# Reordering the entries of the two modulated mixers, their FFNs and the step behind the second gate in a two-network float32 kernel

## The chip, the cores and the metric

The kernel runs on one core of a Trainium2 chip. The metric is the device time of one execution in microseconds (us); the time before is the median of 3 runs. Engines: TensorE (PE, its weight loads PEld), VectorE (DVE), ScalarE (ACT), GpSimd (POOL), and SyncE (SP), which issues the weight transfers.

## The reference

`x` is 512 tokens by 1024. A first network of two layers (half FFN, mixer, half FFN, gate) ends in `rmsnorm(x, final_norm)`; its output is the input of a second network of two layers with modulated norms:

```python
gate = jax.nn.sigmoid(rmsnorm(x, ple_norm[layer]) @ ple_gate[layer])
x = x + gate * (p[layer] @ ple_proj[layer])
...
return rmsnorm(x, final_norm)
# second network, per layer
mod = (c_act @ w_ada[l] + b_ada[l])[:, None, :]
sh1, sc1, g1, sh2, sc2, g2 = jnp.split(mod, N_MOD, axis=-1)
h = rmsnorm_2(x, norm1_w[l]) * (1.0 + sc1) + sh1
x = x + g1 * hybrid_mixer(h, ...)
h = rmsnorm_2(x, norm2_w[l]) * (1.0 + sc2) + sh2
x = x + g2 * swiglu_2(h, w_gate_up[l], w_down[l])
```

## The kernel before

`x` lies in SBUF as 8 tiles of 128 features by 512 tokens. Each float32 product is made of three passes over high and low parts: weights arrive as raw chunks (`raw`, 3 buffers), ACT copies the rounded high part (`wh`), DVE subtracts for the low part (`wl`); both have 3 buffers, so weight tile i can be split only when tile i-3 is used up (`step`). Activations are split in the same way into `hh` and `hl`. Each engine runs one hand-written program in order; a wait on it holds all that stands behind it.

The stages that matter here, in order: `ple 1` (the second gate), `final` (last norm of the first network), `mix2 0`, `ffn2 0`, `mix2 1`, `ffn2 1`. Between stages PE does not wait for the norm. A norm's gain is put into `G`; the first products of the next stage run on `x*G` without the root of the mean square (`gained`), and the root is applied afterwards.

- A second-network mixer is entered by `entered`: four weight tiles T 0 to T 3 (424 columns), each against four token tiles (24 matmuls per weight tile). Meanwhile the squares of x are summed over features by one-column matmuls (`token_means`, 16 of them), DVE copies the sums (`token_roots`), POOL takes the power -0.5 (`roots`, `rtok`), PE spreads the root over the partitions (`along`), and DVE and ACT make eight normed tiles (`modulated`: T from x, G and the root; `hh`; `hl`), which overwrite the gained ones. On DVE, `entered` does the splits for T 0 and T 1 (which reach up to T 3, two ahead) before the copy of the sums, and the split for T 2 (up to the first `xb` tile) before the normed tiles.
- At the entry of `mix2 0` two roots are taken: of the final norm's input (`rtok`, key `al`) and of its output (`r2`, key `al2`, from the squares with the final gain in T1). The final root goes into `R`, and DVE scales the eight tiles of x by it (`rescaled`) inside the mixer's body.
- An FFN of the second network is entered by `opened`: its first two products (w1 0, w1 1) interleaved over the eight gained tiles, with the sums, a two-column product `c` and `along` between them; the third product (w3 0) runs on the normed tiles. The split of w3 1 comes behind the eight normed tiles, in `ffn`.
- `shifted` sums the weight columns times the shift on DVE (for the mixer two per T tile, for the FFN eight in one go).
- `ple` ends with `project`, the additions to x (`add`), the squares and the gained tiles.

The order of the work is the order of the code in each engine's program; there is no planner. Weight transfers are issued by SP when the chunk three before is split.

Of the kernel before, what the change touches and what calls it, by code (L numbers as in the profile page):

```python
# [166 lines left out]
def build(nc, I, out):  # L167
    with ExitStack() as ctx:
# [296 lines left out]
        def pe_program(e):  # L465
# [106 lines left out]
            def entered(s):  # L572
# [3 lines left out]
                for q in range(4):  # L576
# [3 lines left out]
                    for t, b in enumerate(bs):  # L580
                        r = slice(128 * t, 128 * t + 128)
                        for j in range(2):
                            k = 2 * q + j
                            operand((s, "h0"), k)
                            pe.mm(b[:, 0:424], hh[:, k, r], lo[:, j, :], k == 0, False)
                            pe.mm(b[:, 0:424], hl[:, k, r], hi[:, j, :], False, False)
                            done = pe.mm(b[:, 0:424], hh[:, k, r], hi[:, j, :], False, k == 7)
                    done.then_inc(used, g)
                    pe.advance()
                    yield q  # L590
# [6 lines left out]
            def opened(s, names):  # L597
# [7 lines left out]
                for k in range(8):  # L605
# [8 lines left out]
                    if k == 2:  # L614
                        token_means(s)
                    if k == 4:
# [4 lines left out]
                    if k == 5:  # L621
# [3 lines left out]
            def enter(s):  # L625
# [11 lines left out]
                if s[0] == "mix2":  # L637
                    for q in entered(s):
                        if q == 0:
                            token_means(s)  # L640
                        if q == 1:
# [86 lines left out]
            def final(s, nxt):  # L728
                for q in entered(nxt):
                    if q == 1:  # L730
# [4 lines left out]
                    if q == 2:  # L735
                        pe.wait_ge(pooled, ("r2", s))
                        along(("al2", s), r2)
                        pe.wait_ge(pooled, ("rtok", s))
                        along(("al", s), rtok)
# [193 lines left out]
            def mix2(s, nxt):  # L933
# [260 lines left out]
                for j in range(4):  # L1194
# [4 lines left out]
                    done.then_inc(formed, (s, "cat", j))  # L1199
                rest = begin(s, [("out", 0), ("out", 1)], ch, cl, (s, "c"), (0, 1, 2, 3))  # L1200
# [41 lines left out]
        def act_program(e):  # L1242
# [109 lines left out]
            def enter(s):  # L1352
# [16 lines left out]
                for t in range(8):  # L1369
                    modulated(s, 3, t)  # L1370
# [58 lines left out]
            def ple(s, nxt):  # L1429
# [3 lines left out]
                for k in range(8):  # L1433
                    product(s, "gate", k)
                    if k == 7:
                        normed(nxt, 0)
# [12 lines left out]
                for t in (1, 2, 3):  # L1449
                    normed(nxt, t)  # L1450
                squares(nxt, 6)
                for t in (4, 5):
                    normed(nxt, t)
                squares(nxt, 7)
                for t in (6, 7):
                    normed(nxt, t)
                enter(nxt)

            def final(s, nxt):
                entered(nxt)  # L1460
                act.wait_ge(formed, ("al", s))
                act.f(R[:, :], ps(("al", s))[:, :], ACT.Copy).then_inc(left(("al", s)), ("al", s))
# [202 lines left out]
            def mix2(s, nxt):  # L1665
# [216 lines left out]
                for j in range(4):  # L1882
                    act.wait_ge(formed, (s, "cat", j))
                    part((s, "c", j), ps((s, "cat", j))[:, :], ch[:, j, :])
                begin(s, [("out", 0), ("out", 1)])
# [51 lines left out]
        def dve_program(e):  # L1937
# [4 lines left out]
            def shifted(g):  # L1942
# [4 lines left out]
                src = raw_view(n)  # L1947
                for t in rows:
# [14 lines left out]
            def step(g):  # L1963
# [6 lines left out]
                while at[0] < len(order):  # L1970
# [116 lines left out]
            def enter(s):  # L2087
# [17 lines left out]
                for t in modulated(s, 3, R[:, :]):  # L2105
                    pass
# [66 lines left out]
            def out_product(s, nxt, gate=None, rest=False):  # L2173
# [4 lines left out]
                for t in range(8):  # L2178
                    product(s, "out", t)
                    dve.wait_ge(used, G_of[(s, "out", t)])  # L2180
# [6 lines left out]
                    after(nxt, t)  # L2187
                enter(nxt)

            def ple(s, nxt):  # L2190
# [12 lines left out]
                if nxt[0] == "final":  # L2203
# [3 lines left out]
                    dve.tt(G[:, :], G[:, :], cols("final_norm", 0, 8), MUL).then_inc(worked, (to, "G"))  # L2207
                for k in range(8):
                    product(s, "gate", k)
# [13 lines left out]
                    for t in {4: (0, 1), 5: (2, 3), 6: (4, 5)}.get(k, ()):  # L2223
                        add(t)
                        add_square(nxt, t)
                normed = norm_tile if nxt[0] in DEFERRED else gained
# [334 lines left out]
            def mix2(s, nxt):  # L2561
# [36 lines left out]
                if l == 0:  # L2598
                    for t in range(4):
                        rescaled(t)  # L2600
# [22 lines left out]
                if l == 0:  # L2623
                    for t in range(4, 8):
                        rescaled(t)
# [551 lines left out]
```

## Time and profile before

| | us |
|---|---|
| median of 3 runs | 3360.82 (3358.36 to 3363.05) |
| the profiled execution's own time | 3360.46 |
| its span in the profile | 3358.7 |
| PE busy | 3285.3 (98%) |
| DVE busy | 1820.4 (54%) |
| ACT busy | 1167.6 (35%) |
| POOL busy | 74.2 (2%) |

The granted TensorE clock was 0.99 of full on average. PE is busy nearly all the time, so the change can act only on the short stretches where PE is idle or runs at the lower clock. A matmul's busy time overlaps the next one's; the pace is the distance between starts: 0.23 us for 512 columns and 0.19 us for 424 at the full clock.

### The profile page before, as it was taken

Reading aid. Unit: us, or ns where it says so; the run is one execution under the profiler, and the core shown is the slowest. Engines: PE = TensorE matmul, PEld = TensorE weight load, DVE = VectorE, ACT = ScalarE, POOL = GpSimd, SP = SyncE. Lnnn points to the kernel's source line nnn. Section 1 sums busy time; section 2 is a strip of 40 time slices with the busy share of each in tenths; the row PEclk is TensorE's granted clock in tenths of the full one; section 3 lists DMA queues with packets and bytes.
Section 4 is the critical chain, followed back from the end, with each engine's and each line's share of the span. In section 5 each row is a group of like instructions: output and inputs, shape, how many; then the busy total and the mean of one; then the engine's idle time right before and its main releaser. Section 6 shows DMA issues by size and latency. Waiting matters only on the chain.

```text
span 3358.7 us, 37181 instructions
## 1 busy us (share of the span) xinstructions
PE 3285.3 (98%) x15371; PEld 2714.2 (81%) x15371; DVE 1820.4 (54%) x2593; ACT 1167.6 (35%) x1621; POOL 74.2 (2%) x100
## 2 busy tenths in 40 slices
PE   7999999999999999999999999999999999999999
PEld 6888876888888888887888888887788888878887
DVE  5664356566436664366566545876433368563332
ACT  4322253322233222263332224553322245442221
POOL 1000000000000000000000001100000010000000
PEclk9999999999999999999999999999999999999999
DMA  5443321444333443322244332211232322022322
GB/s 152 140 139 121 104 86 51 132 134 148 116 116 101 151 138 116 99 86 76 88 140 149 132 107 84 85 38 38 88 100 86 103 87 76 1 77 99 101 94 69
DMA packets 334142, 339.86 MB, mean 101 GB/s; under 512 B 12182, under 2 KB 329048, under 8 KB 333976
## 3 DMA queue, kind: packets, MB, share of 16 engines
q1 hardware_dynamic: 332696, 333.98, 30.6%
q0 software_dynamic: 1280, 3.50, 0.4%
q8 instruction: 124, 2.03, 0.2%
q14 instruction: 42, 0.34, 0.0%
HBM read 335.36 MB, written 2.10 MB: 100 GB/s over the span
## 4 chain that ended last, share of the span: by engine, by line
PE 62%; DVE 5%; ACT 2%; issue 1%; DVEq 0%; ACTq 0%
PE ps L135 60%; PE ps L138 2%; DVE hl L108 1%; DVE wl L100 1%; DVE ar L100 1%; DVE ar L108 1%; DVE T L108 1%; ACT hh L95 0%; ACT wh L95 0%; DVE ar L117 0%; DVE ada L108 0%; ACT ch L95 0%; ACT ar L95 0%; DVE ar L104 0%; DVE x L100 0%
## 5 line engine op out<-in xcount | busy, mean ns | idle before, releaser
L135 PE MATMUL ps<-hh,wl 128*128 128x512 f32 x2760 | 1091.9, 396 | 30.5 <-DVE wl L100 13.4
L135 PE MATMUL ps<-hl,wh 128*128 128x512 f32 x2760 | 1077.5, 390 | 0.0
L135 PE MATMUL ps<-hh,wh 128*128 128x512 f32 x2760 | 1077.4, 390 | 0.0
L100 DVE TENSOR_TENSOR wl<-raw,wh 128x1024 fp32r<-128x1024 f32 (+2 forms) x547 | 654.0, 1198 | 771.6 <-ACT wh L95 771.3
L95 ACT ACTIVATE wh<-raw 128x1024 fp32r<-128x1024 f32 (+2 forms) x547 | 560.4, 1027 | 481.6 <-PE ps L135 466.8
L135 PEld LDWEIGHTS ps<-hh,wl 128*128 128x128 f32 x2760 | 520.7, 189 | 152.8 <-issue 33.4
L135 PEld LDWEIGHTS ps<-hh,wh 128*128 128x128 f32 x2760 | 520.1, 188 | 110.1
L135 PEld LDWEIGHTS ps<-hl,wh 128*128 128x128 f32 x2760 | 521.1, 189 | 104.1 <-issue 0.6
L135 PE MATMUL ps<-uh,wl 128*128 128x512 f32 x1056 | 411.8, 390 | 0.0
L135 PE MATMUL ps<-uh,wh 128*128 128x512 f32 x1056 | 410.9, 389 | 0.0
L135 PE MATMUL ps<-ul,wh 128*128 128x512 f32 x1056 | 410.8, 389 | 0.0
L95 ACT ACTIVATE uh<-T 128x512 fp32r<-128x512 f32 x132 | 83.5, 633 | 474.6 <-DVE T L100 474.6
L135 PEld LDWEIGHTS ps<-uh,wh 128*128 128x128 f32 x1056 | 198.2, 188 | 41.5
L135 PEld LDWEIGHTS ps<-ul,wh 128*128 128x128 f32 x1056 | 198.2, 188 | 41.0
L135 PEld LDWEIGHTS ps<-uh,wl 128*128 128x128 f32 x1056 | 198.2, 188 | 40.5
L100 DVE TENSOR_TENSOR T<-ps,R 128x512 f32<-128x512 f32 x196 | 134.1, 689 | 121.3 <-PE ps L135 108.1
L95 ACT ACTIVATE T<-T 128x512 f32<-128x512 f32 (+1 forms) x92 | 56.0, 615 | 352.7 <-DVE T L100 352.7
L108 DVE SCALAR_TENSOR_TENSOR ada<-raw,small,ada 128x256 f32<-128x256 f32 x336 | 162.9, 485 | 12.0
L100 DVE TENSOR_TENSOR ul<-T,uh 128x512 fp32r<-128x512 f32 x132 | 91.5, 693 | 92.3 <-ACT uh L95 92.3
L95 ACT ACTIVATE ar<-ar 128x2048 f32<-128x2048 f32 (+6 forms) x68 | 73.2, 1090 | 131.5 <-DVE ar L100 101.8
L135 PE MATMUL ps<-ch,wl 128*128 128x512 f32 x256 | 103.3, 404 | 13.8 <-DVE cl L100 10.3
L135 PE MATMUL ps<-ar 128*128 128x64 f32 (+9 forms) x756 | 111.7, 315 | 4.0 <-DVE ar L108 1.9
(226 smaller groups left out, 2733.2 us busy)
## 6 DMA issues: line engine op xcount, KB each, us to landing
raw<-in_ffn_w SPq DMA_DIRECT2D x120, 1024.0 KB, 5.1
raw<-in_w_ada SPq DMA_DIRECT2D x48, 1024.0 KB, 5.2
raw<-in_w_gate_up SPq DMA_DIRECT2D x44, 1024.0 KB, 5.0
raw<-in_m_w_in SPq DMA_DIRECT2D x26, 1024.0 KB, 5.6
raw<-in_w_down SPq DMA_DIRECT2D x16, 1024.0 KB, 5.2
raw<-in_ffn_w SPq DMA_DIRECT2D x16, 768.0 KB, 4.4
raw<-in_w_in SPq DMA_DIRECT2D x12, 1024.0 KB, 5.3
raw<-in_m_w_out SPq DMA_DIRECT2D x8, 1024.0 KB, 5.2
```

What stands on the lines that cost most here:

```text
L95: return self.issue(lambda e: e.activation(out, in_, func, **kw))
L100: return self.issue(lambda e: e.tensor_tensor(out, a, b, op))
L108: return self.issue(lambda e: e.scalar_tensor_tensor(out=out, in0=a, scalar=s, in1=b, op0=op0, op1=op1))
L135: return self.issue(lambda e: e.matmul(out, l, r, start=start, stop=stop, skip_group_check=True))
L138: return self.issue(lambda e: e.transpose(out, in_, ident))
```

## The change

Five edits. (1) In `opened`, the sums, `c` and the root's spread stand behind k = 0, 1 and 2 of the two products instead of 2, 4 and 5. (2) In the FFN's entry the split of w3 1 stands at normed tile 5 instead of behind tile 7. (3) In the mixers' entries the sums stand after two token tiles of T 0 (mix2 1) or of T 1 (mix2 0), and the root's spread at the end of that weight tile; before, one weight tile later. (4) The end of `ple` is reordered, and for `mix2 0` the shift sums of T 0 to T 3 move into it. (5) The spread of the final root and the scaling of x move from `mix2 0`'s entry and body to its output product, one x tile ahead of each addition.

```diff
@@ PE: entered
+                        if t < 3:
+                            yield q, t
                     done.then_inc(used, g)
                     pe.advance()
-                    yield q
+                    yield q, 3
@@ PE: opened
-                    if k == 2:
+                    if k == 0:
                         token_means(s)
-                    if k == 4:
+                    if k == 1:
                         b = banks.take((s, "c"))
...
-                    if k == 5:
+                    if k == 2:
                         pe.wait_ge(pooled, ("rtok", s))
                         along(("al", s), rtok)
@@ PE: enter
-                    for q in entered(s):
-                        if q == 0:
+                    for at in entered(s):
+                        if at == (0, 1):
                             token_means(s)
-                        if q == 1:
+                        if at == (0, 3):
                             pe.wait_ge(pooled, ("rtok", s))
                             along(("al", s), rtok)
@@ PE: final
-                for q in entered(nxt):
-                    if q == 1:
+                for at in entered(nxt):
+                    if at == (1, 1):
                         token_means(s)
...
-                    if q == 2:
+                    if at == (1, 3):
                         pe.wait_ge(pooled, ("r2", s))
                         along(("al2", s), r2)
-                        pe.wait_ge(pooled, ("rtok", s))
-                        along(("al", s), rtok)
@@ PE: mix2, behind the cat transposes
+                if l == 0:
+                    along(("al", ("final",)), rtok)
@@ ACT: enter (and DVE alike, behind its tile 5)
                 for t in range(8):
+                    if t == 5:
+                        step(G_of[(s, "w1", 1)])
                     modulated(s, 3, t)
@@ ACT: ple
-                        normed(nxt, 0)
+                        for t in range(2):
+                            normed(nxt, t)
...
-                for t in (1, 2, 3):
+                for t in (2, 3):
                     normed(nxt, t)
-                squares(nxt, 6)
-                for t in (4, 5):
-                    normed(nxt, t)
-                squares(nxt, 7)
                 for t in (6, 7):
+                    squares(nxt, t)
+                for t in range(4, 8):
                     normed(nxt, t)
@@ DVE: shifted, step
+                dve.wait_ge(raw_in[n % RAW], n)
...
-                        if o[1] in shift_of:
+                        if o[1] in shift_of and shift_of[o[1]][0] != ("mix2", 0):
                             shifted(o[1])
@@ DVE: out_product
+                    if s == ("mix2", 0):
+                        if t == 0:
+                            rescaled(0)
+                        dve.wait_ge(x_new, (("final",), t))
...
                     after(nxt, t)
+                    if s == ("mix2", 0) and t < 7:
+                        rescaled(t + 1)
@@ DVE: ple
+                    if nxt[0] == "final" and 3 < k < 7:
+                        for q in {4: (0,), 5: (1,), 6: (2, 3)}[k]:
+                            shifted(G_of[(normed_by(nxt), "T", q)])
+                normed(nxt, 1)
+                step(G_of[(s, "gate", 7)])
+                dve.advance()
+                for t in (2, 3):
                     normed(nxt, t)
                 add(6)
-                for t in (4, 5):
-                    normed(nxt, t)
+                add(7)
                 add_square(nxt, 6)
-                add(7)
-                for t in (6, 7):
+                for t in range(4, 8):
                     normed(nxt, t)
@@ DVE: mix2 (and the same for tiles 4 to 7)
-                if l == 0:
-                    for t in range(4):
-                        rescaled(t)
```

How the order of instructions moves, at the three places that matter most.

PE at the entry of `mix2 1`, around the spread of the root (`ident,small`; `wh_63`, `wh_61` and `wh_62` are the high parts of T 0, T 1 and T 2). Before:

```order
L135 MATMUL ps<-wh_61,hl 128x424
L135 MATMUL ps<-wh_61,hh 128x424
L135 MATMUL ps<-ident,small 128x128 x4
L135 MATMUL ps<-wl_65,hh 128x424
L135 MATMUL ps<-wh_62,hl 128x424
```

After:

```order
L135 MATMUL ps<-wh_63,hl 128x424
L135 MATMUL ps<-wh_63,hh 128x424
L135 MATMUL ps<-ident,small 128x128 x4
L135 MATMUL ps<-wl_64,hh 128x424
L135 MATMUL ps<-wh_61,hl 128x424
```

The spread stands behind T 0 and ahead of T 1; before it stood behind T 1. DVE's and ACT's order at this entry is unchanged.

DVE at the end of `ple 1` and in the entry of `mix2 0` (`ada` is a shift sum, `hl` a gained tile's low part, `T_82` the last gate product times its root, `wl_65` the low part of T 1):

```order
+L108 SCALAR_TENSOR_TENSOR ada<-raw_58,mod,ada 128x424 x4
+L108 SCALAR_TENSOR_TENSOR hl<-x,G,hh 128x512
+L100 TENSOR_TENSOR T_82<-ps,R 128x512
+L108 SCALAR_TENSOR_TENSOR hl<-x,G,hh 128x512
 L100 TENSOR_TENSOR wl_65<-raw_60,wh_62 128x848
-L100 TENSOR_TENSOR T_82<-ps,R 128x512
-L108 SCALAR_TENSOR_TENSOR hl<-x,G,hh 128x512 x4
+L108 SCALAR_TENSOR_TENSOR hl<-x,G,hh 128x512 x2
```

Two gained tiles now stand ahead of T 1's split, the first of them ahead of the gate product's T as well, and the shift sums of T 2 and T 3 stand ahead of all of them; before, the split and T came first.

DVE in the output product of `mix2 0`, from the second x tile to the splits behind it (`x<-x,VT,R` is the scaling by the final root, `x<-ps,mod,x` the addition). Before:

```order
L108 SCALAR_TENSOR_TENSOR x<-ps,mod,x 128x512
L108 SCALAR_TENSOR_TENSOR hl<-x,G,hh 128x512
L108 SCALAR_TENSOR_TENSOR acc<-acc,sq_77 128x512
L100 TENSOR_TENSOR wl_65<-raw_59,wh_62 128x1024
L100 TENSOR_TENSOR wl_66<-raw_60,wh_63 128x1024
```

After:

```order
L108 SCALAR_TENSOR_TENSOR x<-x,VT,R 128x512
L108 SCALAR_TENSOR_TENSOR x<-ps,mod,x 128x512
L108 SCALAR_TENSOR_TENSOR hl<-x,G,hh 128x512
L108 SCALAR_TENSOR_TENSOR acc<-acc,sq_77 128x512
L108 SCALAR_TENSOR_TENSOR x<-x,VT,R 128x512
L100 TENSOR_TENSOR wl_65<-raw_59,wh_62 128x1024
L100 TENSOR_TENSOR wl_66<-raw_60,wh_63 128x1024
```

A scaling stands ahead of the addition, and another ahead of the two weight splits.

## Rows read from the trace of the kernel before

**Rows 1.** The page's first part: busy time and share of each engine.

```profile
PE 3285.3 (98%) x15371; PEld 2714.2 (81%) x15371; DVE 1820.4 (54%) x2593; ACT 1167.6 (35%) x1621; POOL 74.2 (2%) x100
```

**Rows 2.** Timeline, `mix2 0` entry: start, duration, instruction, idle before it and releaser.

```profile
2083.27 0.39 PE L135 MATMUL ps<-ch,ul 128*128 128x512 f32 x1
...
2088.33 0.74 DVE L108 SCALAR_TENSOR_TENSOR hl<-x,G,hh 128x512 fp32r<-128x512 f32 x1
2089.22 0.43 PE L135 MATMUL ps<-wl,hh 128*128 128x424 f32 x1 [3.07 <-DVE hl L108]
...
2102.64 1.93 PE L135 MATMUL ps<-ones,T 128*128 128x1 f32 x16
...
2107.27 0.16 DVE L111 COPY small<-ps 128x4 f32<-128x4 f32 x1
2107.57 2.14 POOL L100 TENSOR_TENSOR small<-small 128x4 f32<-128x4 f32 x2 [11.72 <-DVE small L111]
2111.27 1.95 PE L135 MATMUL ps<-ident,small 128*128 128x128 f32 x16
2112.36 1.41 DVE L108 SCALAR_TENSOR_TENSOR T<-x,G,ps 128x512 f32<-128x512 f32 x2 [3.51 <-PE ps L135]
...
2128.72 3.52 PE L138 MATMUL ps<-ident,ar 128*128 128x128 f32 x16 [1.89 <-DVE ar L108]
```

**Rows 3.** Timeline, `mix2 1` entry.

```profile
2727.63 0.91 ACT L95 ACTIVATE wh<-raw 128x848 fp32r<-128x848 f32 x1 [0.46 <-PE ps L135]
2729.66 1.36 DVE L108 SCALAR_TENSOR_TENSOR ada<-raw,mod,ada 128x424 f32<-128x424 f32 x2
2731.89 0.15 DVE L111 COPY small<-ps 128x4 f32<-128x4 f32 x1
2732.19 1.01 POOL L100 TENSOR_TENSOR small<-small 128x4 f32<-128x4 f32 x1 [373.86 <-DVE small L111]
2733.83 1.05 PE L135 MATMUL ps<-ident,small 128*128 128x128 f32 x8
2736.33 1.40 DVE L108 SCALAR_TENSOR_TENSOR T<-x,G,ps 128x512 f32<-128x512 f32 x2
```

**Rows 4.** Timeline, `ffn2 0` entry.

```profile
2351.62 0.47 PE L135 MATMUL ps<-hh,wl 128*128 128x512 f32 x1 [0.93 <-DVE wl L100]
2354.40 1.22 DVE L100 TENSOR_TENSOR wl<-raw,wh 128x1024 fp32r<-128x1024 f32 x1 [0.20 <-ACT wh L95]
2357.01 0.16 DVE L111 COPY small<-ps 128x4 f32<-128x4 f32 x1 [1.39 <-PE ps L135]
2361.46 1.05 PE L135 MATMUL ps<-ident,small 128*128 128x128 f32 x8
2363.18 1.41 DVE L108 SCALAR_TENSOR_TENSOR T<-x,G,R 128x512 f32<-128x512 f32 x2 [2.84 <-ACT R L95]
...
2372.68 1.63 DVE L108 SCALAR_TENSOR_TENSOR hl<-T,mod,hh 128x512 fp32r<-128x512 f32 x2
...
2378.64 0.76 PE L135 MATMUL ps<-hh,wl 128*128 128x512 f32 x1 [3.24 <-DVE wl L100]
```

**Rows 5.** Windows: length, busy PE, PEld, DVE, ACT, POOL, granted clock, DMA.

```profile
2378.60:2381.60 3.00, 2.96 (x7) 2.40 (x8) 2.30 (x3) 1.34 (x2) 0.00 (x0) 0.52 0.61 203
2752.70:2757.00 4.30, 4.30 (x20) 3.77 (x21) 4.08 (x6) 4.26 (x6) 1.76 (x2) 0.60 0.46 138
1043.70:1048.00 4.30, 4.30 (x27) 3.83 (x27) 1.74 (x2) 2.61 (x3) 0.00 (x0) 1.00 0.01 4
```

**Rows 6.** Timeline, scaling of x in `mix2 0`'s body, then its output product.

```profile
2132.71 2.73 DVE L108 SCALAR_TENSOR_TENSOR x<-x,VT,R 128x512 f32<-128x512 f32 x4
...
2321.15 2.36 DVE L100 TENSOR_TENSOR wl<-raw,wh 128x1024 fp32r<-128x1024 f32 x2
2322.53 0.47 PE L135 MATMUL ps<-ch,wl 128*128 128x512 f32 x1 [0.51 <-DVE wl L100]
```

**Rows 7.** Timeline, entry of the FFN behind `ple 0`.

```profile
1043.70 0.47 PE L135 MATMUL ps<-hh,wl 128*128 128x512 f32 x1 [1.74 <-DVE hl L108]
```

More of the change, by code:

```diff
@@ L1460, in final @@
                 entered(nxt)
-                act.wait_ge(formed, ("al", s))
-                act.f(R[:, :], ps(("al", s))[:, :], ACT.Copy).then_inc(left(("al", s)), ("al", s))
             def root(key, n):
@@ L1884, in mix2 @@
                     part((s, "c", j), ps((s, "cat", j))[:, :], ch[:, j, :])
+                if l == 0:
+                    key = ("al", ("final",))
+                    act.wait_ge(formed, key)
+                    act.f(R[:, :], ps(key)[:, :], ACT.Copy).then_inc(left(key), key)
                 begin(s, [("out", 0), ("out", 1)])
@@ L2105, in enter @@
                 for t in modulated(s, 3, R[:, :]):
-                    pass
+                    if t == 5:
+                        step(G_of[(s, "w1", 1)])
             def output():
@@ L2207, in ple @@
                     dve.tt(G[:, :], G[:, :], cols("final_norm", 0, 8), MUL).then_inc(worked, (to, "G"))
+                normed = norm_tile if nxt[0] in DEFERRED else gained
                 for k in range(8):
-                    product(s, "gate", k)
+                    if k < 7:
+                        product(s, "gate", k)
+                    else:
+                        normed(nxt, 0)
                     dve.wait_ge(used, G_of[(s, "gate", k)])
@@ L2222, in ple @@
                             dve.tt(cl[:, c, :], ps((s, "pt", c))[:, :], ch[:, c, :].bitcast(F32), SUB).then_inc(lo_part, (s, "p", c))
-                    for t in {4: (0, 1), 5: (2, 3), 6: (4, 5)}.get(k, ()):
+                    pair = {4: (0, 1), 5: (2, 3), 6: (4, 5)}.get(k, ())
+                    for t in pair:
                         add(t)
+                    for t in pair:
                         add_square(nxt, t)
-                normed = norm_tile if nxt[0] in DEFERRED else gained
-                for t in range(4):
+                    if nxt[0] == "final" and 3 < k < 7:
[5 more added lines that the diff above has]
+                for t in (2, 3):
                     normed(nxt, t)
                 add(6)
-                for t in (4, 5):
-                    normed(nxt, t)
+                add(7)
                 add_square(nxt, 6)
-                add(7)
-                for t in (6, 7):
+                for t in range(4, 8):
                     normed(nxt, t)
@@ L2597, in mix2 @@
                 convolved(0)
-                if l == 0:
-                    for t in range(4):
-                        rescaled(t)
                 for c in (2, 0, 1):
@@ L2622, in mix2 @@
                 conv_from(1)
-                if l == 0:
-                    for t in range(4, 8):
-                        rescaled(t)
                 step(G_of[(s, "qu", 0)])
```

## The prediction

> **What bounds the kernel now.** I read the page first: TensorE is busy for 98% of the span [rows 1], so a change of order can win only where TensorE idles or runs at half clock. Then I read, per engine, the timeline of each stretch that the diff touches, looking at the idle time before each matmul and what ended it. There are five such stretches.
>
> In the entry of `mix2 0`, TensorE starts the last two projections at 2083.27 (12 matmuls of 0.23 us, so 2.7 us), then idles 3.07 us for the first gained tile, is slow a little later, and idles again for 1.89 us until 2128.72, where DVE's T rows are missing; these hang on the normed tiles, and the normed tiles on the root, which TensorE spreads only at 2111.27 [rows 2]. In the entry of `mix2 1` the same chain runs from the split of T 3 to the root and the normed tiles [rows 3]. In the entries of the two FFNs the root is spread at 2361.46, the first normed tile is begun at 2363.18, the eighth is done at about 2374.3, and the fourth product starts only at 2378.64 after 3.24 us idle, since its low part is split behind the normed tiles [rows 4]; the second FFN repeats this pattern. Behind the first gate there is one idle stretch of 1.74 us [rows 7].
>
> **The clock.** Two idle stretches were followed by half clock: 3.24 us idle by a granted clock of 0.52 over 3 us, and 1.89 us idle (after a stretch of small waits) by 0.60 over 4.3 us. After 1.74 us idle it stayed 1.00 [rows 5]. So I count a new idle stretch of 2 us or more with 0 to 1.7 us of slow matmuls on top (0.48 x 3.0 = 1.4, 0.40 x 4.3 = 1.7), a long one with the whole.
> The Trainium skill (TensorE: Matmul & The Clock Gate, HAM oscillation — how this bites in real kernels) says that the clock falls after long idle gaps of TensorE, not short ones. By that rule only the long gap of part 3 would carry the surcharge and the sum below would be about 2 us lower; the row at 1.89 us speaks against taking it so.
>
> **1, FFN entries (edits 1 and 2), twice.** TensorE's work stays. The sums come after k = 0. Two interleaved products cost 6 x 0.23 = 1.36 us per k. From the start at 2351.6 the sums could begin at 2352.4, and wait some 0.4 us for the last square. DVE copies them behind its split of w3 0, which lasts from 2354.40 to 2355.6 [rows 4], so at 2355.7 instead of 2357.01; POOL needs 1.0 us [rows 3], so the root is there at 2357, before TensorE gets to the spread behind k = 2 (2352.8 + 1.7 sums + 2 x 1.36 + 0.4 for c = 2357.7). The spread is then 3.7 us earlier than 2361.46, and the first normed tile starts at 2359.5. Eight tiles at 1.32 us each (from 2363.18 to 2374.3 [rows 4]) now contain the split of w3 1, 1.2 us. They end at 2371.7. TensorE ends the two opened products at 2365.6, catches up with tiles 5 to 7, and is done with w3 0 at 2372.5; w3 1 is split by then. It starts 6.1 us earlier than 2378.64 and without the half clock (1.7 us): -7.8 us. Bounds: -5.5 (a spread only as much earlier as the copy, 1.3 us, still removes the 3.24 idle and its clock, 0.6 from shorter waits) to -8.5. Next in line is w1 2's split, behind two activations, some 2 us ahead of its use. For both FFNs: -15.6 us.
>
> **2, mix2 0's entry (edits 3 and 4).** The last gate product ends at 2083.27, when the gained tiles may be written. ACT takes 0.7 us for each and DVE 0.74 [rows 2]; with two of them ahead of the split of T 1, the low parts are there by 2084.9 and 2086.1, and TensorE, done with the projections at 2086.0, goes on without the 3.07 us. T 0 ends at 2090.9. T 1 up to its second tile ends at 2093.2; 8 square sums and 8 more of T1 follow, 1.7 + 1.9 us [rows 2], then two tiles, 2.3 us: 2099.2. Here it wants r2. DVE has four gained tiles and the splits of T 2 and T 3 ahead of the copy; I get the copy at 2098.8 instead of 2107.27, then POOL 2.1 us and 0.3 of latency [rows 2]: 2101.3. So 2.2 us idle, a new wait. The spread of one root (0.9 of the 1.95 us, the other moves) ends at 2102.3, and the normed tiles start 10.0 us earlier than 2112.36. T 2 and T 3 are over by 2111.8 (2113.3 with slow matmuls), so the tiles' buffers come free in time. The transposes now at 2128.72 start at 2118.6, -10.1 us, and run at 1.6 to 3.2 us instead of 3.2, of which I take -1.2. The moved spread comes back in the mixer with 0.9 us of TensorE time. Together -10.4 us. Bounds: -6 (the copy 4 us later than I count) to -12.
>
> **3, mix2 1's entry (edit 3).** DVE's and ACT's order is unchanged there: the copy of the sums stands behind the split of T 3, and T 3's buffer is free only when T 0 is used up. Now TensorE asks for the root at exactly that moment. The way from there is 0.2 + 0.91 (ACT) + 2.23 (DVE from 2729.66 to the copy) + 0.3 + 1.01 (POOL) + 0.1 = 4.8 us [rows 3]. Before, T 1's 24 matmuls (4.7 us) covered it; now TensorE idles. It also waits 0.7 us for the last square, since the sums come 2.3 us earlier, and the spread (0.8 us from 2733.83, half of the two spreads' 1.95) is now ahead of T 1's end. T 1's end frees the buffer of the xb tile, whose split stands ahead of the normed tiles: 2733.83 to 2736.33 [rows 3]. So the normed tiles, and with them the whole chain to the transposes, come 4.8 + 0.7 + 0.8 = 6.3 us later, and 1.7 us more by the half clock: +8.0 us. Bounds: +6.3 to +8.5; 0 if the root were there.
>
> **4, the scaling in the output product (edit 5).** 8 x 0.68 = 5.4 us of DVE [rows 6] leave the body, where TensorE waited for nothing of theirs: 0. In the output product the first is hidden under the wait for the first product. The next two (1.33 us) stand ahead of the split that TensorE already waits for until 2322.53 [rows 6]: +1.3 us, an idle stretch of 2.2 us. DVE then catches up, 1.2 us per product. The last two stand ahead of w1 1's split, for which TensorE waits until 2351.62 [rows 4]: +1.3 us, and 2.3 us idle with 0.6 more for the square behind it. Clock: 0 to 3.4, I take 2.4, the second being likelier. +5.0 us; bounds 0 (DVE has slack) to +6.
>
> **5, behind the first gate (edit 4).** The idle 1.74 us [rows 7] is split up: w1 1's low part now stands behind two gained tiles and comes 0.8 us late, and tiles 4 to 7 behind the last addition make TensorE wait 1.3 us at k = 4. +0.2 us; bounds -1.0 to +1.5.
>
> **Sum.** -15.6 - 10.4 + 8.0 + 5.0 + 0.2 = -12.8 us against the profiled execution's own 3360.46 (span 3358.7 and 1.8 around it), which is 0.36 below the median 3360.82. So 3360.8 - 12.8 = 3348.0 us.
>
> **Rivals.**
> - A, the second mixer's wait is covered (chance 0.11): if the copy could pass T 3's split, -20.8 us, 3340. For it: before, the root was ready 0.5 us ahead of need. Against it: the copy stands behind the split on an in-order engine.
> - B, DVE's slack absorbs the scalings (0.13): -17.8 us, 3343. For it: DVE is busy 54% [rows 1]. Against it: the two splits named are already what TensorE waits for.
> - C, the first mixer's root comes late (0.15): four gained tiles, two splits and the POOL additions of squares are all ahead of the copy, and each us of delay shifts the chain by one. With 4 to 5 us, 3352.5.
> - D, slower (0.05): the normed tiles overwrite gained ones that the opened products still read. If the `hh` writes had to wait until those are over, the earlier root would bring nothing in both FFNs: no 15.6 us, +2.8 us, 3363.6. It decides once the eighth tile ends after 2373.5 plus 3 us of w3 1's split. Against it: PE reports each k as it is used, and the root reaches DVE when k = 3 is over.
>
> The forecast itself has 0.56, own range 3344 to 3352.
>
> **Range and chances.** 0.2% (6.7 us, below 3354.1) is what a measurement of this kernel can tell from no change. Forecast, A and B are faster (0.80), of C about a quarter is (0.04), and the rest of C and a stray case are same (0.11); D is slower (0.05). The range 3340 to 3355 leaves out the far end of A and all of D.
>
> **What would show it.** Right: an idle stretch of 4 to 5 us before `ident,small` in `mix2 1`'s entry, released by POOL, with the transposes behind it some 8 us later in the stage; one of about 2 us before it in `mix2 0`'s; w3 1 without idle before it; idle of 2 us or more before the output product's fourth tile and w1 1 in `mix2 0`, and the old 0.9 in `mix2 1`. Wrong: any of the FFN entries still idle behind w3 0, or the normed tiles of `mix2 0` less than 6 us earlier.

## The result and the profile after

The changed kernel takes 3366.2 us (median of 17 runs, 3364.3 to 3370.9) against 3360.4 us for the kernel before (17 runs on the same chip): ratio 1.0019, 95% interval 1.0012 to 1.0027. I forecast 3348.0 us and a range of 3340 to 3355. It is no faster; by the bound of 0.2% it counts as the same, and the interval says slightly slower.

The page of the changed kernel, first part, beside [rows 1]:

```profile
PE 3292.2 (98%) x15371; PEld 2725.7 (81%) x15371; DVE 1823.2 (54%) x2593; ACT 1167.1 (35%) x1621; POOL 75.8 (2%) x100
```

PE is busy 6.9 us longer with the same number of instructions: the loss shows first as slower matmuls. The span went from 3358.7 to 3364.6 us, and I split it at fixed rows of PE's timeline. The second column is the kernel before; "FFN only", "bank", "root back", "scaling back", "both back" and "k = 1" are experiments of the next section. Lengths in us:

```
stage                              before  after   FFN    bank   root  scaling both   k = 1
                                                   only          back  back    back
start to spread in ple 1           2046.1  2046.6  2049.1 2044.5 2046.1 2046.0 2050.0 2045.2
... to T 0 of mix2 0                 43.2    41.7    43.2   41.7   41.7   41.7   41.7   41.7
T 0 to end of transposes             42.7    44.0    42.1   37.8   43.1   38.8   38.8   38.8
body of mix2 0                      168.0   171.9   171.5  168.2  171.7  171.6  171.6  171.6
output product of mix2 0             50.0    51.5    50.4   51.5   53.3   51.1   51.0   51.0
ffn2 0 to T 0 of mix2 1             373.0   371.3   367.3  370.3  370.3  367.4  367.4  365.2
T 0 to end of transposes, mix2 1     32.4    40.7    32.8   40.7   32.2   40.6   31.6   33.2
body of mix2 1                      170.5   169.8   170.5  169.8  170.4  169.9  167.8  170.6
output product of mix2 1             50.9    50.7    50.5   50.7   51.1   50.6   51.1   50.0
ffn2 1 to the end                   382.1   376.3   376.2  376.3  376.3  376.3  376.3  374.1
```

Three of these stages (the start and both bodies) move by 3 to 6 us between profiled executions of identical code: "FFN only" has the code of before in the first two and shows 2049.1 and 171.5 us where before has 2046.1 and 168.0. Together they are 3.8 us longer in the profile after, 6.5 in "FFN only" and 2.9 in "k = 1". What moves in them is time at half clock. The body of `mix2 0` as a window of its own, in the kernel before, after, and in "FFN only" (the last columns are granted clock, DMA share and GB/s):

```profile
2131.89:2299.87 167.98, 166.92 (x987) 140.01 (x985) 125.59 (x213) 89.76 (x188) 6.56 (x8) 0.98 0.16 50
2132.35:2304.26 171.91, 170.75 (x995) 144.01 (x993) 124.66 (x208) 92.86 (x192) 6.94 (x8) 0.96 0.14 44
2134.34:2305.83 171.49, 170.45 (x987) 143.29 (x985) 126.95 (x213) 90.54 (x189) 6.56 (x8) 0.96 0.16 50
```

0.02 of 170 us is 3.4 us, nearly the whole difference of 3.5 and 3.9. Why one execution gets more of it than another stays open, and so does whether an edit further ahead can bring it about. I read every edit in the other stages, which scatter less but not by nothing: the output product of `mix2 0` took 50.0 to 51.1 us with the code of before, and 51.5 and 53.3 us with the changed code ("root back" has half clock there behind the same idle 2.0 us). In these stages together the changed kernel is 2.1 us longer, not 12.8 shorter.

Over the whole span the mean granted clock fell from 0.990 to 0.986: TensorE stood at half clock for 68 us before and for 92 us after. Half of the 24 us more, 12 us, is the most that this can have cost. By stage it is 7.3 us more in the entry of `mix2 0`, 6.4 in its body, 6.8 in `ffn2 0`, 5.1 in the entry of `mix2 1`, and 1.7 less in the rest.

In `mix2 0`'s entry after the change (PE, DVE and POOL of the timeline):

```profile
2083.91 3.60 DVE L108 SCALAR_TENSOR_TENSOR ada<-raw,mod,ada 128x424 f32<-128x424 f32 x4
2087.42 0.75 DVE L108 SCALAR_TENSOR_TENSOR hl<-x,G,hh 128x512 fp32r<-128x512 f32 x1
2088.32 0.43 PE L135 MATMUL ps<-wl,hh 128*128 128x424 f32 x1 [1.59 <-DVE hl L108]
...
2102.27 0.15 DVE L111 COPY small<-ps 128x4 f32<-128x4 f32 x1
2102.57 2.12 POOL L100 TENSOR_TENSOR small<-small 128x4 f32<-128x4 f32 x2 [6.26 <-DVE small L111]
2106.52 1.05 PE L135 MATMUL ps<-ident,small 128*128 128x128 f32 x8
2109.02 1.40 DVE L108 SCALAR_TENSOR_TENSOR T<-x,G,ps 128x512 f32<-128x512 f32 x2
...
2122.88 2.35 DVE L108 SCALAR_TENSOR_TENSOR ar<-ps,small,ar 128x424 f32<-128x424 f32 x4
2123.58 0.79 PE L135 MATMUL ps<-hh,wl 128*128 128x512 f32 x1 [6.03 <-DVE ar L108]
```

Against [rows 2] the root does come earlier (the copy at 2102.27 instead of 2107.27, the normed tiles at 2109.02 instead of 2112.36). Then the first xb product waits 6.03 us, an idle stretch that the kernel before does not have, and its releaser is DVE's first copy of a T tile out of PSUM, which is no operand of it: it looks like a wait for a PSUM bank, and experiments 1 and 2 test that. The transposes follow at 2130.69, later than the 2128.72 of before.

PE in the output product of the first mixer and in the second mixer's entry, after the change:

```profile
2328.47 0.47 PE L135 MATMUL ps<-ch,wl 128*128 128x512 f32 x1 [2.00 <-DVE wl L100]
...
2358.87 0.66 PE L135 MATMUL ps<-hh,wl 128*128 128x512 f32 x1 [2.27 <-DVE wl L100]
...
2739.02 2.08 PE L135 MATMUL ps<-ident,small 128*128 128x128 f32 x8 [4.56 <-POOL small L100]
...
2766.10 1.94 PE L138 MATMUL ps<-ident,ar 128*128 128x128 f32 x16 [1.90 <-DVE ar L108]
```

Here the predicted waits are there: 4.56 us for POOL's root, and 2.00 and 2.27 us for low parts where [rows 6] and [rows 4] have 0.51 and 0.93. The old 3.24 us ahead of the fourth product are gone. The granted clock (the figure behind POOL) of three windows:

```profile
2102.20:2106.50 4.30, 4.30 (x13) 4.04 (x14) 0.38 (x3) 0.00 (x0) 3.20 (x5) 0.51 0.58 187
2123.50:2127.00 3.50, 3.42 (x8) 2.74 (x9) 2.93 (x5) 0.00 (x0) 3.03 (x7) 0.52 0.00 0
2356.00:2370.00 14.00, 11.73 (x43) 9.69 (x42) 5.59 (x9) 3.01 (x4) 1.01 (x1) 0.63 0.23 75
```

The second and third hold what follows the idle 6.03 and 2.27 us. The first follows no idle stretch but 32 one-column sums, behind which the kernel before has half clock too, for half as long (windows after, then before):

```profile
2099.60:2106.40 6.80, 6.80 (x26) 6.54 (x26) 2.98 (x6) 1.51 (x2) 3.20 (x5) 0.50 0.37 118
2105.00:2108.40 3.40, 3.36 (x10) 3.18 (x11) 3.21 (x6) 0.00 (x0) 0.83 (x1) 0.50 0.00 0
```

### The profile page after: what moved, and what is told of

It is laid out like the page before. It is cut to its first block, busy times and chain, and to the rows that moved or that the text cites. A ratio compares the mean times of both kernels' runs of the same rounds, so it can differ in the third digit from the quotient of the medians.

```text
span 3364.6 us, 37195 instructions
## 1 busy us (share of the span) xinstructions
PE 3292.2 (98%) x15371; PEld 2725.7 (81%) x15371; DVE 1823.2 (54%) x2593; ACT 1167.1 (35%) x1621; POOL 75.8 (2%) x100
## 4 chain that ended last, share of the span: by engine, by line
PE 89%; DVE 7%; ACT 2%; issue 1%; DMA 0%; SPq 0%; POOL 0%; DVEq 0%; ACTq 0%; POOLq 0%
PE ps L135 88%; PE ps L138 2%; DVE wl L100 1%; DVE ar L100 1%; DVE hl L108 1%; DVE ar L108 1%; ACT wh L95 1%; DVE T L108 1%; ACT ar L95 0%; ACT hh L95 0%; DVE ada L108 0%; DVE ar L117 0%; ACT ch L95 0%; DMA raw<-in_ffn_w 0%; DVE ar L104 0%
```

## The experiments

**1. One bank further.** The kernel has 8 PSUM banks handed out in turn. Edit 5 takes one spread out of the entry, and with it one turn of this rotation: the first xb product, on bank 3 before, is now on bank 5, where T 0 lies until DVE has copied it behind all normed tiles. The experiment turns the rotation on by six at that place and changes nothing else of the changed kernel:

```diff
                         along(("al2", s), r2)
+                banks.turn += 6
```

> The changed kernel (span 3364.6) with one line more in TensorE's program: behind the root's spread in mix2 0's entry six PSUM banks are skipped, so that the first xb product takes the bank of the square sums (ps3), as in the kernel before, and not T 0's (ps5), which DVE empties only behind all normed tiles. Theory (bank): the idle stretch of 6.03 us ahead of that product goes; the product is then paced by the normed tiles, which end at 2122.4, and the transposes come at about 2125.3 instead of 2130.7: 5 to 6 us less in this stage, whole kernel about 3361. Rival (the wait is for the normed tiles or T rows themselves): no change of the place of the transposes, whole kernel about 3366.

Measured: 3357.54 us, ratio to before 0.9993 (0.9984 to 1.0002), by the ratios 8.7 us less than the changed kernel. The transposes in PE's timeline:

```profile
2122.22 1.94 PE L138 MATMUL ps<-ident,ar 128*128 128x128 f32 x16 [1.89 <-DVE ar L108]
```

The stage from T 0 to their end is 37.8 us instead of 44.0: the bank is worth 6.2 us here. The idle 1.89 us ahead of the transposes are those of before.

**2. The bank in the kernel before.** Two runs turn the rotation in the kernel before, where nothing else is changed. In the first I miscounted: by seven banks the product falls on the bank of the second spread, which ACT empties, and not on T 0's.

```diff
                         pe.wait_ge(pooled, ("rtok", s))
                         along(("al", s), rtok)
+                banks.turn += 7    # the second run: += 2
```

> The kernel before with nothing changed but the rotation of the PSUM banks: seven banks are skipped behind the first mixer's last spread, so that the first xb product takes the bank it takes in the changed kernel, T 0's. Theory, the bank alone makes the wait: xb starts when DVE has copied T 0, at some 2126.9 us instead of 2118.6 us, TensorE is idle for about 8 us, the transposes behind it start at 2134 us instead of 2128.7 us and, since their operands are then long there, run at 1.9 us instead of 3.5 us; the stage from the row to the body is 18 to 19 us long instead of 14.2, +4 to +5 us in all, 3365 us. Rival, the wait for DVE in the changed kernel comes from the earlier root or from DVE's new order and not from the bank: no idle stretch there, and the time of before.

> The kernel before with nothing changed but the rotation of the PSUM banks: two banks are skipped behind the first mixer's last spread, so that the first xb product takes T 0's bank and the four transposes the banks that they take in the changed kernel. Theory, T 0's bank alone makes the wait: DVE begins its four copies of T at 2126.2 us as before, xb starts some 0.7 us behind that instead of at 2118.6 us, after 8 us of idle time released by DVE; its 24 matmuls take 7.1 us as in the changed kernel, the transposes start at 2134 us instead of 2128.7 us and take 1.6 us less: the stage from the row to the body is 18 us long instead of 14.2 (16.7 with the spread's bank), +3.8 us, 3364 us. Rival, DVE does not release it: the stage stays at 14.2 us.

Measured: 3363.93 us with seven (1.0007, 0.9999 to 1.0016), 3371.20 us with two (1.0032, 1.0020 to 1.0044), where I had expected 3364. The first xb product in PE's timeline, in the one and in the other:

```profile
2125.31 0.80 PE L135 MATMUL ps<-hh,wl 128*128 128x512 f32 x1 [6.95 <-ACT R L95]
```

```profile
2127.58 0.79 PE L135 MATMUL ps<-hh,wl 128*128 128x512 f32 x1 [8.38 <-DVE ar L108]
```

With T 0's bank the product waits for DVE's copy in the kernel before too, and the stretch from the row product (`ada,small`, behind T 3) to the body grows from 14.2 to 19.4 us (16.7 with the other bank). So a late bank alone makes the wait, without the earlier root or DVE's new order; the rest of that run's 9.9 us lies outside the entry, 3.5 of it in the body that scatters.

**3. The second mixer's root put back** (sums and spread one weight tile later, the changed kernel otherwise).

```diff
-                        if at == (0, 1):
-                            token_means(s)
                         if at == (0, 3):
+                            token_means(s)
+                        if at == (1, 3):
                             pe.wait_ge(pooled, ("rtok", s))
```

> The changed kernel with the sums and the root's spread of mix2 1's entry put back by one weight tile (sums behind T 0, spread behind T 1). Theory: the copy of the sums stands behind T 3's split, which waits for T 0's end; the 4.6 us idle ahead of the spread goes, with the half clock behind it, and the stage is 8 us shorter (3358 for the whole). Rival (the earlier spread pays back part of it further on, in the mixer's body): under 6 us.

Measured: 3354.58 us (0.9988, 0.9979 to 0.9998). T 0 to the row product is 21.19 us again, as before, against 29.43: edit 3 costs 8.2 us there, and I had said 8.0. The rival, a part paid back further on, did not appear: the stage to the end of the transposes is 32.2 us, with 32.4 before.

**4. The FFN entries alone** (edits 1 and 2 in the kernel before), then each of the two alone.

> The kernel before with edits 1 and 2 alone (sums, c and spread at k = 0, 1, 2 of the opened products; split of w3 1 at normed tile 5). Theory: both FFN entries gain what the second one gained in the changed kernel, 5.9 us each, since w1 1's idle time ahead of the sums is 0.9 us as there: 3360.4 - 11.8 = 3348.6. Rival (the half clock that the changed kernel shows over 10 us in the first FFN's entry comes from the early one-column sums, not from the longer idle time that edit 5 makes): the first FFN gains under 3 us, 3351.5 or more.

> The kernel before with edit 1 alone: in the FFN entries the sums follow k = 0, c follows k = 1, the spread k = 2; w3 1's split stays behind all eight normed tiles. Theory, root and split are two links of one chain: the tiles start about 3.5 us earlier and w3 1's split with them, and TensorE is done with w3 0 only 1 to 2 us earlier, so the idle 3.24 us shrinks to 1 or less: -3.5 us for each FFN, -7.0 us, 3353.8 us. Rival, the earlier root is worth nothing while the split stands behind the tiles: 0 to -2 us.

> The kernel before with edit 2 alone: w3 1's split stands ahead of normed tile 5 on ACT and DVE, the root stays at its old place. Theory: w3 1 starts without its 3.24 us of idle time and the half clock behind it, but tiles 5 to 7 come 1.2 us later and TensorE, which follows them, with them: -3.2 us for each FFN, -6.4 us, 3354.4 us. If -3.5 and -3.2 add up to more than the 5.7 measured for both edits, each of the two alone removes most of the idle stretch and its half clock, which I had counted whole beside the earlier root. Rival, the split alone does it all and the earlier root nothing: -5.7 for each FFN, 3349.4 us.

Measured: both 3352.76 us (0.9974, 0.9965 to 0.9984); sums alone 3362.98 (0.9997, 0.9988 to 1.0007); split alone 3359.05 (0.9995, 0.9986 to 1.0004). By the stages of `ffn2 0` and `ffn2 1` both edits save 5.6 and 5.9 us, the sums alone 0.7 and 0.6, the split alone 2.2 and 3.9 (I had expected 3.2 each, and 3.5 each for the sums). The medians show less: for both edits I had expected 3348.6 us. Four of the ten executions took 3345.7 to 3346.8 us at a mean granted clock of 0.990, the other six 3351.9 to 3355.7 us at 0.987 or 0.988, so the scatter that goes with the clock shows within one kernel too. My expectation for the sums alone fell: the tiles start 1.9 us earlier, but the idle stretch keeps its whole length, since the split of w3 1 starts behind the last tile whenever that is, and the matmuls behind it are slow for longer. From PE's timeline and the windows of that run:

```profile
2382.71 0.76 PE L135 MATMUL ps<-hh,wl 128*128 128x512 f32 x1 [3.23 <-DVE wl L100]
```

```profile
2361.00:2366.00 5.00, 5.00 (x21) 4.22 (x20) 0.83 (x3) 0.00 (x0) 1.01 (x1) 0.66 0.18 60
2382.70:2388.00 5.30, 5.29 (x13) 4.13 (x14) 3.52 (x4) 1.58 (x2) 0.00 (x0) 0.50 0.60 198
```

The window from 2361 shows the other half of the story: the clock is 0.66 right behind the one-column sums. Experiment 7 takes that up.

**5. The scaling put back** (edit 5 undone: the final root's spread again beside the other one, `rescaled` again in the body).

```diff
                         along(("al2", s), r2)
+                        pe.wait_ge(pooled, ("rtok", s))
+                        along(("al", s), rtok)
```

> The changed kernel without edit 5: the final root is spread right behind r2 in mix2 0's entry and x is scaled in the mixer's body. This also moves the bank rotation back by one, so the xb product does not take T 0's bank. Theory: the bank wait goes (5 to 6 us), the output product loses its two longer idle stretches (2.9 us), the spread in the half-clock stretch behind the cat transposes goes (2.0, of which 0.9 comes back in the entry) and the first FFN's entry gains 3 us more: 3366 - 12.5 = 3353.7. Rival (DVE's 5.4 us in the body now delay something, or the half clock stays in the first FFN's entry): 3357 or more.

Measured: 3354.28 us (0.9986, 0.9976 to 0.9995). I had expected 3353.7 us. This also restores the bank rotation, so its 11 us less than the changed kernel (by the ratios) hold both: T 0 to the transposes' end is 38.8 us instead of 44.0, and `ffn2 0` 4.0 us shorter.

**6. Both put back, and the shift sums.** The changed kernel without edit 5 and with the second mixer's root at its old place; and the same with only two of the four shift sums moved into `ple`.

```diff
-                        for q in {4: (0,), 5: (1,), 6: (2, 3)}[k]:
+                        for q in {4: (0,), 5: (1,), 6: ()}[k]:
```

> The changed kernel without edit 5, and with the sums and the spread of the second mixer's entry back at their old places (the first mixer's entry and both FFN entries stay changed). Theory, each cost hangs on its own stage: the entry of `mix2 0` keeps the 5.3 us of the earlier root since the second spread moves the rotation of the PSUM banks on, the second mixer's entry is 8 us shorter than in the changed kernel, the output product loses its two idle stretches (4 us); both FFN entries keep 5.7 us each. Sum against the kernel before: -0.6 (behind ple 1) - 4.7 - 11.4 = -16.7 us, 3342.5 us. Rival, the stages trade with each other (half clock that goes in one comes back in the next, as the 64-column part of the first mixer's body already does by 3.5 us): 3347 to 3350 us.

> The kernel of the run above, with the shift sums of T 2 and T 3 back at those tiles' splits and only those of T 0 and T 1 ahead in `ple`. Theory, DVE's 3.60 us of four shift sums ahead of the first gained tile are what makes hl 2.5 us later than I predicted: two of them gone, the gap of 1.59 us before T 0 goes, and the way from the last projections to T 0 is about 1.6 us shorter, and the copy of the sums is not later, since TensorE's sums come after T 1's tiles: 1 to 1.6 us less than the run above. Rival, DVE's queue between T 0 and the copy of the sums is what sets the root: the two shift sums come back ahead of the copy, the root is 1.8 us later and the time is the same or up to 1 us more.

Measured: 3344.23 us (0.9956, 0.9943 to 0.9968) and 3349.49 us (0.9967, 0.9955 to 0.9980). The first is 14.8 us less than before by the ratio, and the median lies between the theory's 3342.5 and the rival's 3347; in the stages outside the three scattering ones it is 16.3 us less, with 16.7 forecast. In the second the gap before T 0 is gone (the stage to T 0 is 39.9 us instead of 41.7), but the two shift sums now stand ahead of the copy, and PE waits for the root, as its timeline shows:

```profile
2108.44 3.78 PE L135 MATMUL ps<-ident,small 128*128 128x128 f32 x16 [3.33 <-POOL small L100]
```

T 0 to the transposes' end is 40.9 us instead of 38.8. The two stages together are 0.4 us longer and not 1 to 1.6 shorter: the rival holds, and DVE's queue ahead of the copy sets the root in that run. Of the 5.3 us between the medians the spans show 3.1, of which 2.5 lie in the three scattering stages.

**7. The sums one step later.** In the run with both put back, PE's rows around the sums of `ffn2 0`, and two windows, are

```profile
2354.96 0.47 PE L135 MATMUL ps<-hh,wl 128*128 128x512 f32 x1 [0.94 <-DVE wl L100]
...
2356.24 0.35 PE L135 MATMUL ps<-ones,acc 128*128 128x1 f32 x2 [0.35 <-issue]
...
2362.93 1.05 PE L135 MATMUL ps<-ident,small 128*128 128x128 f32 x8
```

```profile
2353.60:2358.00 4.40, 3.12 (x21) 2.28 (x21) 2.89 (x5) 2.19 (x3) 0.00 (x0) 1.00 0.43 139
2358.00:2363.00 5.00, 5.00 (x19) 4.14 (x19) 1.19 (x3) 0.00 (x0) 1.01 (x1) 0.66 0.25 87
```

One run puts a second step of 512-column matmuls between the idle 0.94 us and the sums (its diff against the run with both put back is below); another has the sums behind k = 2, with c and the spread behind k = 3:

```diff
-                    if k == 0:
-                        token_means(s)
                     if k == 1:
+                        token_means(s)
+                    if k == 2:
                         b = banks.take((s, "c"))
```

> The kernel with edit 5 and the second mixer's root put back, and in the FFN entries the sums one product step later, behind k = 1, with c and the spread behind k = 2. There the sums behind k = 0 followed idle stretches of 0.93 and 0.35 us within 1.3 us, TensorE was busy 3.12 of 4.40 us around them, and the granted clock was 0.66 over the 5 us behind, so the spread came 9.7 us behind the stage's start, where I had predicted 7.9. Theory, the half clock comes from one-column sums right behind the idle stretches: with a whole k = 1 between them the clock stays at 1.00, the spread comes at 7.9 us, and each FFN is 1.8 us shorter by that and by up to 1.3 us less of slow matmuls: -4 to -5 us against the run with both put back, about 3340 us. Rival, the sums themselves bring the half clock wherever they stand before k = 2: the spread comes at 10 us, and the time is the same to 1 us longer.

> As the run above, but with the sums behind k = 2, where they stand in the kernel before (whose granted clock there is 1.00), and c and the spread both behind k = 3. By either theory the clock stays at 1.00 behind the sums. The spread then comes at the stage's start + 8.9 to 9.3 us (2.7 us earlier than the 11.6 of before, less what POOL's root, done at 8.5 us, makes it wait), against 9.7 with the early sums: each FFN is 0.5 us shorter by the spread and up to 1.3 us by the clock, 1 to 3.5 us in all less than the run with both put back. If the rival for the half clock holds, this run is the shortest of the three; by the theory the one with the sums behind k = 1 is.

Measured: 3340.80 us (0.9939, 0.9926 to 0.9953) and 3347.96 us (0.9960, 0.9947 to 0.9972). Behind k = 1 the clock stays full and the spread comes 7.4 us behind the stage's start, not 9.7 (row and window of that run):

```profile
2355.78 1.14 PE L135 MATMUL ps<-ident,small 128*128 128x128 f32 x8
```

```profile
2353.00:2358.00 5.00, 5.00 (x34) 4.54 (x35) 1.85 (x4) 0.60 (x1) 1.01 (x1) 1.00 0.28 96
```

The FFN stages are then 7.8 and 8.0 us shorter than before, and this is the shortest kernel of the study, 0.6% faster than before. With the sums behind k = 2 the spread comes at 8.8 us and the stages are 6.4 and 5.2 us shorter; the second has 3.4 us at half clock from the end of w3 0 on, the first none, with the same code in both. I had expected this run to be 1 to 3.5 us shorter than the one with both put back: it is 1.0 us shorter in the stages outside the three, and 1.3 us longer by the ratios. The theory for the half clock held, in every profile of this study: in all 16 FFN entries with the sums behind k = 0 (eight kernels, the changed one among them; three of the entries have 2.27 us of idle time ahead) half clock is there within 3 us of the first sum, and in none of the 13 with the sums behind k = 1 or 2 and 0.93 us of idle time ahead. Both kernels beat the one before and the changed one.

**8. The scaling's price by itself.** Edit 5 in again in that shortest kernel, with the rotation turned on by six as in experiment 1.

> The shortest kernel so far (sums behind k = 1 in the FFN entries, edit 5 and the second mixer's root put back) with edit 5 in again, and the banks turned on by six behind the first mixer's entry, so that the wait for T 0's bank does not come with it. This is edit 5's price by itself. Theory: the entry is 1 us shorter, since one spread leaves it, the spread costs 2 us behind the cats, w1 1 in `mix2 0` waits 2.3 us instead of 0.9 with up to 1.7 us of half clock behind it, and the fourth output tile 2.0 us: +3 to +5 us, 3344 to 3346 us. My prediction's term was +5.0 with 0.9 for the spread counted elsewhere. Rival, the half clock was by chance and DVE's slack takes the scalings: within 1 us of 3340.8 us.

Measured: 3342.11 us (0.9945, 0.9931 to 0.9958), 1.3 us more (2.0 by the ratios), and the intervals overlap. That is below the 3 to 5 us that I expected and hardly above the rival's 1 us. The theory's costs are there (`ffn2 0` +2.9 us, with 2.27 us idle and a granted clock of 0.52 behind it, the output product +0.4, less than that stage scatters), its gain was larger than I said (the entry -1.7 us, one spread of two gone), and the spread at the end of the body cost nothing I can see (171.5 against 171.6 us, in a stage that scatters by more than the 2 us expected). PE at w1 1, and the window behind it:

```profile
2350.66 0.71 PE L135 MATMUL ps<-hh,wl 128*128 128x512 f32 x1 [2.27 <-DVE wl L100]
```

```profile
2350.60:2354.00 3.40, 3.34 (x8) 2.73 (x9) 1.90 (x3) 2.19 (x3) 0.00 (x0) 0.52 0.70 214
```

## Why the prediction was wrong

**The step that failed** is in part 2: "T 2 and T 3 are over by 2111.8 (2113.3 with slow matmuls), so the tiles' buffers come free in time. The transposes now at 2128.72 start at 2118.6". I followed the SBUF buffers and the root, and not the PSUM bank of the first product behind the row. T 0's bank is emptied only behind the normed tiles (copies from 2122.88). The transposes came at 2130.69. The entry (ple 1 to the transposes' end) changed by -0.1 us where I had -10.4 (with the moved spread's 0.9); with the bank moved it changed by -6.4 (experiment 1), at the near end of my bounds of -6 to -12.

**The rest of that term's size** is a root that came too late, rival C's case in part, and that through half clock and DVE's queue. The normed tiles started 3.3 us earlier than before (2109.02 against 2112.36) where I had 10.0, and less than 6 was one of my signs of a wrong forecast. The copy came at 2102.27 and not 2098.8, and PE took the spread at 2106.52, 5.1 us later than I had worked out (2101.4). It did so without idling, since its own matmuls were late as well, so the predicted wait of 2.2 us did not appear. Experiment 1 has nearly the same root (the spread comes 17.2 us behind T 0, 18.2 in the changed kernel, 22.1 before) and still gains 6.4 us, so it is the bank that made the term nothing. Three things I had not counted: the gap before T 0 shrank to 1.59 us instead of nothing, since the two additions of squares take 2.63 us there (below) and four shift sums, 3.60 us, stand ahead of the first gained tile; half clock lay under part of T 0 and under T 1's sums and the matmuls behind them (0.50 over 6.8 us), and I had allowed 1.5 us for it (2113.3 for 2111.8); and the normed tiles wait for the split of xb's tile, 1.23 us of DVE from 2107.87 on, whose high part comes only then.

**Part 1**, -15.6 us, measured -11.5 (5.6 + 5.9). The mechanism held, its size not. The failed term is the spread, "3.7 us earlier": it came 1.9 us earlier, because the sums stood 1.3 us behind an idle stretch and half clock followed them. Without it (experiment 7) both stages save what I had said, 7.8 and 8.0. In the whole changed kernel `ffn2 0` shows only -1.6, since edit 5's idle 2.27 us at w1 1 lie at its start and the clock of the window from 2356 is 0.63.

**Part 3**, +8.0, measured +8.2, with the predicted wait (4.56 against 4.8 us), its releaser and the late transposes. Rival A did not appear.

**Part 4**, +5.0, has the predicted waits at the two predicted places (2.00 and 2.27 us for 2.2 and 2.3), but measured +3.3 for them (2.9 + 0.4, experiment 8) and +1.3 in the whole kernel. Its clock term was right in kind: 2.27 us idle were followed by 0.52 over 3.4 us, and the 2.00 us by full clock (by half clock in experiment 3). The idle time before the fourth tile cost little, as DVE's slack came back within the product.

**Part 5**, +0.2, which no run measures, since it lies in the start that scatters: the 1.74 us of [rows 7] became 0.69 and 1.03 us of PE's timeline:

```profile
1035.50 0.47 PE L135 MATMUL ps<-hh,wl 128*128 128x512 f32 x1 [0.69 <-DVE wl L100]
1041.54 0.47 PE L135 MATMUL ps<-hh,wl 128*128 128x512 f32 x1 [1.03 <-DVE hl L108]
```

**The sum with the measured terms**: -11.5 - 0.1 + 8.2 + 3.3 + 0.2 = +0.1 us, where the stages outside the three show +2.1 and the medians +5.8. What is between these is not settled: 3.8 us lie in the three scattering stages, as time at half clock, whose length differs between executions of identical code, and I made no run that holds them still. That the changed kernel is not faster needs none of them; that it is slower may rest on them. Rival D's mechanism, the only slower one I gave, did not appear. The range was too narrow on the slow side, because no bound of part 2 allowed the earlier root to be worth nothing.

## What to carry to other kernels

Where buffers are handed out in turn, an operation that leaves also shifts the buffer of everything behind it. Follow the first product behind it to the bank it gets and to who empties that bank, as a term of the sum. One line that skips banks showed it, and was worth 6.2 of the 6.4 us that the entry then gained.

An earlier root or split gains only up to the next queue: look at what stands ahead of the copy on the in-order engine, and at what is idle just before one-column matmuls. Where two kernels differ by 0.2%, compare their stages and the granted clock in each before the medians: 3.4 us of one body came and went with the clock alone.

## What the runs showed of the hardware

- One-column sums of 1.8 us right behind idle stretches of 0.94 and 0.35 us were followed by a granted clock of 0.66 over 5 us; the same sums one step of 1.36 us later were followed by 1.00, with the first idle stretch, 0.93 us, ahead as well (experiment 7). The 32 one-column sums of `mix2 0`'s entry had no idle stretch in the 7 us ahead of them, and half clock came with them all the same: over 6.8 us in the changed kernel, from 2 us behind the first sum on, and over 3.4 us in the kernel before, right behind the last.
- An idle stretch of 8.38 us was followed by a granted clock of 0.56 over 7 us (experiment 2), and one of 1.89 us before the same 16 transposes was followed once by half clock (3.52 us for them, [rows 2]) and once not (1.94 us, experiment 1). The 2.0 us ahead of the output product's fourth tile were followed by 1.00 in the changed kernel and by 0.50 over 3.4 us in experiment 3, with the same code there.
- DVE's two additions of squares took 2.63 us where POOL was adding squares too, and one took 0.69 us while a POOL addition that started in the same moment took 1.84 us. Timeline of DVE and of POOL after the change:

```profile
2081.17 1.30 POOL L100 TENSOR_TENSOR T<-T,T 128x512 f32<-128x512 f32 x1 [5.46 <-ACT T L95]
2081.18 2.63 DVE L100 TENSOR_TENSOR acc<-acc,sq 128x512 f32<-128x512 f32 x2
...
2094.46 1.84 POOL L100 TENSOR_TENSOR T<-T,T 128x512 f32<-128x512 f32 x1 [9.50 <-ACT T L95]
2094.47 0.69 DVE L100 TENSOR_TENSOR acc<-acc,sq 128x512 f32<-128x512 f32 x1
```

In the first pair DVE loses the length of one POOL addition (2.63 = 1.30 + 2 x 0.67), in the second POOL loses most of the length of DVE's (1.84 = 1.30 + 0.54, of 0.69). The Trainium skill (SBUF — State Buffer, Who interferes with whom) says that such instructions, with two inputs in SBUF on DVE's side, take turns on a shared port and one blocks until the other is done. These rows agree with that.
